# Causal mask of both attentions: from TensorE products to one fused VectorE pass

## The chip, the cores and the metric

The kernel runs on one core of a Trainium2 chip. The metric is the device time of one execution in microseconds, as the median of several runs. The engines of the core work in parallel, each in its own program order: TensorE (PE in the profile, its weight loads PEld), VectorE (DVE), ScalarE (ACT), GpSimd (POOL) and SyncE (SP), which issues most of the DMAs. They wait for one another by counting semaphores that the kernel sets.

## The reference

A decoder trunk of two layers, 512 tokens of width 1024, everything in float32. A layer projects the normalised input to four token mixers (a block attention A, an RWKV-7 recurrence B, a gated spatial unit C and a differential attention D), projects their outputs back, and adds a mixture of 32 experts. The change concerns the scores of A and D:

```python
# A: with 512 tokens in blocks of 256 and up to 3 past blocks chosen, every past block is
# chosen, so this is plain causal attention with 4 heads of width 64
mask = mc[..., None] & (kpos <= pc[None, None, :, None, None])
s = jnp.where(mask, s, -jnp.inf)
p = softmax(s)

# D: two score maps of width 32 for each of 4 heads
mask = jnp.arange(end)[None, :] <= (q0 + jnp.arange(DIFF_Q_BLOCK))[:, None]
p = jax.nn.softmax(jnp.where(mask, s, -jnp.inf), axis=-1)
attn = p[:, :, 0] - lam * p[:, :, 1]
out = attn @ v
```

## The kernel before

Each layer has a projection stage, a mixer stage, the output projection with the routing, and the experts. In the mixer stage the function `mixer_steps` writes out by hand one order for all engines. It goes through the RWKV steps of two channel halves, c = 0 and c = 1. For each half these are P (products within a chunk), T (turns), V (a triangular solve of 16 x 16 blocks on VectorE, followed by a DMA round trip of the blocks through DRAM), L (merging of blocks), four times Z, B, S (the recurrence over chunks), F and, for c = 1, G (the end). Between these steps it places the units of the attentions, by the list `UNITS_PER_STEP`: A has 16 units (4 query tiles i of 128 rows times 4 heads) and D 16 more. A unit of tile i has w = 128 (i + 1) key columns. Units A0 to A6 lie beside the last steps Z to F of the first half, A7 to A10 beside P, A11 and A12 beside T, A13 on and D0 beside V, D1 to D3 beside L, D4 to D15 beside the steps Z, B, S of the second half. Each engine issues its part of the step and then its part of the unit. The steps V, Z and B of the second half also hold products on TensorE whose result is not used (`keep_busy`, L592).

In the function `attn` every engine does its share of unit u, and, behind it, of the units u - 1 and u - 2:

- TensorE: scores of unit u into one of two PSUM banks (L721; for D two maps, one in each bank, behind each other), the mask as a product of the identity and the constant `causal`, added to the diagonal block of the bank (L724; for D twice, after both maps), then the turning of the probabilities of unit u - 1 (L731), then the product with V of unit u - 2 (L743). The scores of u wait until the exponential has read the bank.
- VectorE: for unit u - 1 the reciprocal of the sums (L1395), for D also the combination of the two maps (L1398, L1400, L1401); then the negated maximum of unit u (L1408), once per map; then the output of unit u - 2 (L1415 for A, L1417 for D).
- ScalarE: the exponential of unit u with that maximum as bias, with the sum of the row as accumulator output (L1091), then the copy of the turned probabilities (L1099).

Before unit 0 of each attention TensorE turns the queries and keys (L707) and ScalarE copies them (L1081). From then on the key columns of the token buffer `TK[0]` are no longer read. GpSimd applies the rotary embedding to the inputs of D (L1713 to L1718) and later writes two identity buffers for the second half (L1736), waiting for the last output of the first half. SyncE fetches the expert weights: `fill(0)` after the second DMA round trip of the blocks, the next ones after `mixed_done`, which VectorE gives after the end of attention D, and most of them after the output projection.

Of the kernel before, what the change touches and what calls it, by code (L numbers as in the profile page):

```python
# [14 lines left out]
P = 128  # L15
# [42 lines left out]
    fin_inA=4, fin_psA=3, fin_sqA=1, y_doneA=1, fin_inD=4, fin_psD=3, fin_sqD=1, y_doneD=1,  # L58
    mixed_done=1, mt_ps=6, mt_a=4, mt_v=2, res_ps=8, res_added=8, n2_squares=4, n2_turned=4, n2_copied_a=4, n2_copied_v=4,
    logits=4, exp_in=2, exp_done=2, chosen=2, ranks=2, routed=2, xt_ps=15, xt_copied=16, gate_ps=32, up_ps=32, gated=32, hidden=32,  # L60
    ht_ps=32, ht_copied=32, y2_ps=32, y2_copied=33, combined=8, first_hot=4, picked=3, lam_rt=3, sgu_done=1)

OV_ADDS = dict(ov_in=(0, 48), ov_used=(2, 1), ov_made=(6, 7), ov_ps=(0, 15), ov_gated=(0, 1), ov_copied=(0, 6), ov_added=(5, 8))

# [21 lines left out]
def build(nc, x, w_in, w_out, pcol, prow, w2a2, g2, sguT, router, norm2_g, w_gate, w_up, w_down,  # L86
          final_g, cf, cm, out):
    ctx = ExitStack()
    with ctx:
# [47 lines left out]
        def cst(name):  # L137
            lo, n = CF[name]
            return CFs[:, lo:lo + n]
# [32 lines left out]
        QKV = {"A": TK[0], "D": TK[2]}  # L172
        BLOCK_TO = [TK[0], TK[1], TK[3], TK[2]]
        VAD, UV = TK[1], TK[3]
        XS = XSb[:, :].rearrange("p (g t) -> p g t", g=8)
        AR = view(SC, 0, 2048, "p (c m w t) -> p c m w t", c=2, m=4, w=2)
        BT = view(SC, 2048, 1024, "p (c t) -> p c t", c=2)
# [114 lines left out]
        extra_full = [sem(f"extra_full{m}") for m in range(4)]  # L292
        combined = sem("combined")
        first_hot, picked = sem("first_hot"), sem("picked")
        lam_rt, sgu_done = sem("lam_rt"), sem("sgu_done")

# [68 lines left out]
        with nc.Block() as block:  # L367
# [143 lines left out]
            def _(pe):  # L511
# [4 lines left out]
                for layer in range(DEPTH):  # L516
# [180 lines left out]
                    def attn(m, u):  # L697
# [12 lines left out]
                        if u < 16:  # L710
                            i, h = unit_of[u]
                            w = (i + 1) * P
                            for a in range(nm):
                                n = u if m == "A" else 2 * u + a
                                if n >= 2:
                                    pe.wait_ge(*at(layer, s["exped"], n - 1))
                                if m == "A":
                                    rows = slice((h % 2) * 64, (h % 2) * 64 + 64)
                                else:
                                    rows = slice((h % 2) * 64 + a * 32, (h % 2) * 64 + a * 32 + 32)  # L720
                                mm(PS[5 + n % 2][:, 0:w], QKT[rows, h // 2, i * P:w], QKT[rows, 2 + h // 2, 0:w], start=True, stop=False)  # L721
                            for a in range(nm):
                                n = u if m == "A" else 2 * u + a
                                mm(PS[5 + n % 2][:, i * P:w], ident, cst("causal"), start=False, stop=True).then_inc(s["scores"], 1)  # L724
                        if 1 <= u <= 16:
                            i, h = unit_of[u - 1]
                            pe.wait_ge(*at(layer, s["exped"] if m == "A" else s["probs"], u))
# [228 lines left out]
            def _(act):  # L956
# [25 lines left out]
                for layer in range(DEPTH):  # L982
# [92 lines left out]
                    def attn(m, u):  # L1075
                        s, nm = mix[m], 2 if m == "D" else 1
                        if u == 0:
                            scale = float(HD) ** -0.5 if m == "A" else 32.0 ** -0.5
                            for j in range(4):
                                act.wait_ge(*at(layer, s["qk_ps"], j + 1))  # L1080
                                ac(QKT[:, j, :], PS[5 + j % 2][:, :], ACT.Copy, scale=scale if j < 2 else 1.0).then_inc(s["qk_copied"], 1)  # L1081
                        if u < 16:
                            i, h = unit_of[u]
                            w = (i + 1) * P
                            if u >= 2:
                                act.wait_ge(*at(layer, s["pt_ps"], u - 1))
                            for a in range(nm):
                                n = nm * u + a
                                col = (0 if m == "A" else 16) + n
                                act.wait_ge(*at(layer, s["maxed"], n + 1))  # L1090
                                ac(PB[:, u % 2, a, 0:w], PS[5 + n % 2][:, 0:w], ACT.Exp, bias=nmx[:, col:col + 1],  # L1091
                                   accum_out=sums[:, col:col + 1]).then_inc(s["exped"], 1)
                        if 1 <= u <= 16:
                            i, h = unit_of[u - 1]
                            w = (i + 1) * P
                            act.wait_ge(*at(layer, s["pt_ps"], u))
                            if u >= 3:
                                act.wait_ge(*at(layer, s["o_ps"], u - 2))
                            ac(PT[:, (u - 1) % 2, 0:w], PS[7][:, 0:w], ACT.Copy).then_inc(s["pt_copied"], 1)  # L1099
# [47 lines left out]
            def _(dve):  # L1147
# [47 lines left out]
                for layer in range(DEPTH):  # L1195
# [191 lines left out]
                    def attn(m, u):  # L1387
# [14 lines left out]
                        if u < 16:  # L1402
                            i, h = unit_of[u]
                            w = (i + 1) * P
                            for a in range(nm):
                                n = nm * u + a
                                dve.wait_ge(*at(layer, s["scores"], n + 1))
                                V.tensor_reduce(nmx[:, base + n:base + n + 1], PS[5 + n % 2][:, 0:w], AX.X, ALU.max, negate=True).then_inc(s["maxed"], 1)  # L1408
                        if u >= 2:
                            n = u - 2  # L1410
                            i, h = unit_of[n]
# [281 lines left out]
            def _(pool):  # L1693
# [11 lines left out]
                for layer in range(DEPTH):  # L1705
# [25 lines left out]
                    pool.wait_ge(*at(layer, proj_copied, copied("t", (3, NT - 1))))  # L1731
                    pool.wait_ge(*at(layer, sgu_ps, 1))
                    rope("D", SC0 + 11136, 16, 4)
                    pool.wait_ge(*at(layer, mix["A"]["y_ps"], 4))
                    for buf in (DB, EB):
                        G.tensor_copy(buf, eye).then_inc(mix["D"]["eye"], 1)  # L1736
# [133 lines left out]
```

## Time and profile before

| | us |
|---|---|
| median of 3 runs | 1950.47 (1950.07 to 1953.31) |
| the profiled execution, its own time | 1947.54 |
| its span in the profile, first to last instruction | 1945.7 |
| TensorE busy, whole span | 1665.0 |
| VectorE busy | 620.4 |
| ScalarE busy | 277.4 |
| GpSimd busy | 153.6 |

All times within the profile count from the start of the span. The mixer stage of layer 0 lies at about 228 to 375, that of layer 1 at about 1191 to 1338. An engine row gives start and duration of an instruction or of a group that follows without a break; what stands in brackets is the idle time of the engine just before it and the instruction whose end ended that idle time.

### The profile page before, as it was taken

The page shows a single profiled execution, that of the slowest core. Times are in us where ns is not written, and L with a number is a line of the kernel's source. Part 1 is how long each engine was busy: PE and PEld are TensorE (multiplying, and loading weights), DVE is VectorE, ACT ScalarE, POOL GpSimd, SP SyncE. Part 2 cuts the span into 40 slices and gives each one's busy share as a digit, 9 for nine tenths or more (in the row PEclk, how much of TensorE's full clock was granted, in tenths as well). Part 3 has the DMA queues.
Part 4 walks back from the last instruction along what each step waited for, and adds up shares of the span by engine and source line. Part 5 has one row for each costly group of instructions (what it writes and reads, how often), then busy time and mean ns, then how long its engine had stood idle before and what let it go on. Part 6 is the DMA issues. An engine that isn't in the chain of part 4 may idle for free.

```text
span 1945.7 us, 22555 instructions
## 1 busy us (share of the span) xinstructions
PE 1665.0 (86%) x9440; PEld 1005.9 (52%) x9440; DVE 620.4 (32%) x1397; ACT 277.4 (14%) x636; POOL 153.6 (8%) x171
## 2 busy tenths in 40 slices
PE   7999878899998878977599998788999988788872
PEld 4445557557665445544244465565576644455441
DVE  2164265715121113111313633566241211131113
ACT  2211233311000000000113113332100000000001
POOL 0010100002111110100001001000031111101100
PEclk9999999898999999999799999898989999899996
DMA  9212001056999999999822020101489999999994
GB/s 303 87 45 93 1 9 44 1 246 271 423 424 425 425 423 397 422 425 425 336 80 92 6 89 1 52 1 71 194 346 423 424 423 424 425 398 425 425 423 186
DMA packets 72772, 492.93 MB, mean 253 GB/s; under 512 B 24964, under 2 KB 26948, under 8 KB 36833
## 3 DMA queue, kind: packets, MB, share of 16 engines
q1 hardware_dynamic: 62592, 475.10, 59.4%
q0 software_dynamic: 10080, 16.41, 2.3%
q8 instruction: 75, 1.23, 0.3%
q14 instruction: 25, 0.20, 0.0%
HBM read 479.58 MB, written 28.11 MB: 261 GB/s over the span
## 4 chain that ended last, share of the span: by engine, by line
PE 62%; DMA 24%; DVE 7%; SPq 3%; issue 2%; ACT 1%; DVEq 0%; POOLq 0%; ACTq 0%
PE banks L844 13%; PE banks L552 12%; DMA RING<-in_w_up 8%; PE banks L859 7%; PE banks L797 6%; PE banks L541 6%; DMA RING<-in_w_down 6%; DMA RING<-in_w_gate 5%; DMA SCAN<-in_w_down 4%; PE banks L822 2%; PE banks L721 2%; SPq L434 2%; PE banks L743 1%; PE banks L632 1%; PE banks L649 1%
## 5 line engine op out<-in xcount | busy, mean ns | idle before, releaser
L844 PE MATMUL banks<-RING,XS 128*64 128x256 f32 x2816 | 326.5, 388 | 47.9 <-DMA RING<-in_w_up 31.2
L844 PEld LDWEIGHTS banks<-RING,XS 128*64 128x64 f32 x2816 | 224.8, 140 | 160.9 <-DMA RING<-in_w_up 42.2
L552 PE MATMUL banks<-RING,XNT 128*128 128x512 f32 x512 | 227.1, 601 | 0.2 <-DMA RING<-in_w_in_blocks 0.2
L859 PE MATMUL banks<-RING,XS 128*64 128x512 f32 x736 | 168.1, 597 | 26.9 <-issue 14.4
L1589 DVE SCALAR_TENSOR_TENSOR XS<-banks,TABLE,XS 128x256 f32<-128x256 f32 x60 | 29.0, 484 | 453.8 <-PE banks L844 453.3
L552 PEld LDWEIGHTS banks<-RING,XNT 128*128 128x128 f32 x512 | 97.8, 193 | 119.7 <-issue 118.6
L1130 ACT ACTIVATE XS<-banks,TABLE 128x256 f32<-128x256 f32 x60 | 28.5, 474 | 816.3 <-PE banks L844 816.3
L1780 POOL DMA_INDIRECT y_rows<-XS,SOLVE x64 | 64.9, 1014 | 631.1 <-DVE XS L1626 617.5
L844 PE MATMUL banks<-TOK,XS 128*64 128x256 f32 x768 | 92.5, 397 | 25.7 <-DMA SCAN<-in_w_down 11.1
L859 PEld LDWEIGHTS banks<-RING,XS 128*64 128x64 f32 x736 | 58.0, 136 | 105.2 <-issue 105.2
L1626 DVE COPY XS<-banks 128x512 f32<-128x512 f32 x64 | 44.2, 691 | 210.4 <-PE banks L859 210.4
L541 PE MATMUL banks<-XNT,RING 128*128 128x512 f32 x256 | 110.2, 592 | 0.0
L844 PEld LDWEIGHTS banks<-TOK,XS 128*64 128x64 f32 x768 | 63.7, 144 | 57.1 <-issue 23.0
L797 PE MATMUL banks<-RING,XNT 128*128 128x512 f32 x192 | 90.4, 617 | 1.4 <-ACT XNT L1104 1.4
L541 PEld LDWEIGHTS banks<-XNT,RING 128*128 128x128 f32 x256 | 48.6, 190 | 61.2 <-issue 61.2
L1091 ACT ACTIVATE XNT<-banks,SMALL 128x128 f32<-128x128 f32 (+3 forms) x96 | 50.1, 525 | 132.8 <-DVE SMALL L1408 127.6
L797 PEld LDWEIGHTS banks<-RING,XNT 128*128 128x128 f32 x192 | 37.1, 199 | 44.6 <-issue 42.4
L1408 DVE TENSOR_REDUCE SMALL<-banks 128x1 f32<-128x128 f32 (+3 forms) x96 | 44.1, 486 | 31.1 <-PE banks L724 30.2
L850 PE MATMUL banks<-CF,XS 128*128 128x128 f32 x132 | 30.2, 310 | 27.0 <-DVE XS L1589 23.4
L721 PE MATMUL banks<-XNT 32*128 32x128 f32 (+7 forms) x192 | 50.8, 476 | 2.7 <-ACT XNT L1081 2.7
L1354 DVE COPY_PREDICATED RING<-CM,banks 128x512 f32<-128x512 uint8 x40 | 29.2, 729 | 73.7 <-PE banks L647 43.1
L1744 POOL DMA_INDIRECT slot_table<-SMALL,SOLVE x16 | 15.8, 989 | 457.3 <-DVE SOLVE L1573 453.1
(312 smaller groups left out, 1950.8 us busy)
## 6 DMA issues: line engine op xcount, KB each, us to landing
RING<-in_w_up SPq DMA_DIRECT2D x46, 2048.0 KB, 27.4
RING<-in_w_down SPq DMA_DIRECT2D x46, 2048.0 KB, 27.2
RING<-in_w_gate SPq DMA_DIRECT2D x42, 2048.0 KB, 29.6
TOK<-in_w_gate SPq DMA_DIRECT2D x14, 2048.0 KB, 28.5
RING<-in_w_in_blocks SPq DMA_DIRECT2D x12, 2048.0 KB, 9.6
TOK<-in_w_up SPq DMA_DIRECT2D x10, 2048.0 KB, 33.4
TOK<-in_w_down SPq DMA_DIRECT2D x8, 2048.0 KB, 30.5
SCAN<-in_w_gate SPq DMA_DIRECT2D x6, 2048.0 KB, 19.0
```

The source lines that it names most:

```text
L434: sp.dma_start(dst, src.rearrange("a p n -> p (a n)")).then_inc(full, 16)
L541: last = mm(bank[:, :], w[:, k, j * P:(j + 1) * P], XNT[:, k, :], start=(k == 0), stop=(k == KD - 1))
L552: last = mm(bank[:, :], XNT[:, k, i * P:(i + 1) * P], w[:, k, :], start=(k == 0), stop=(k == KD - 1))
L721: mm(PS[5 + n % 2][:, 0:w], QKT[rows, h // 2, i * P:w], QKT[rows, 2 + h // 2, 0:w], start=True, stop=False)
L797: last = mm(PS[4 * n + i][:, :], src[:, i * P:(i + 1) * P], w[:, k, :], start=(k == 0), stop=(k == KD - 1))
L822: last = mm(PS[k // 4][:, (k % 4) * P:(k % 4 + 1) * P], X3[:, i, :].rearrange("t (p k) -> t p k", k=KD)[:, :, k], HOT[:, i, :], start=(i = ...
L844: last = mm(bank[f * CAP:(f + 1) * CAP, 0:256], rows[:, k, :], w[:, k, f * 256:(f + 1) * 256], start=(k == 0), stop=(k == KD - 1))
L859: last = mm(PS[5][n * CAP:(n + 1) * CAP, :], HT[:, j, f * CAP:(f + 1) * CAP], w[:, k, n * BN:(n + 1) * BN], start=(k == 0), stop=(k == KF ...
L1091: ac(PB[:, u % 2, a, 0:w], PS[5 + n % 2][:, 0:w], ACT.Exp, bias=nmx[:, col:col + 1], accum_out=sums[:, col:col + 1]).then_inc(s["exped"], 1)
L1408: V.tensor_reduce(nmx[:, base + n:base + n + 1], PS[5 + n % 2][:, 0:w], AX.X, ALU.max, negate=True).then_inc(s["maxed"], 1)
L1626: V.tensor_copy(YS[h], PS[5][:, :]).then_inc(y2_copied, 1)
L1780: pool.indirect_dma_start(y_halves, bass.IndirectOffsetOnAxis(ap=YROW[:, e:e + 1], axis=0), YS[h], None, bounds_check=4 * SEQ - 1, oob_is_ ...
```

## The change

The mask is no longer added by TensorE. The scores close their accumulation with the product L721 itself, so each map counts as ready by itself. VectorE runs one instruction per map over the bank: it adds a mask read from SBUF, multiplies by -1, writes the result back in place into PSUM, and folds the minimum of what it writes into the [128, 1] column that held the negated maximum before. The exponential reads the negated scores with a scale of -1. The mask is a tile of 4 blocks of 128 columns, three of zeros and one causal block, laid in the first key columns of `TK[0]`; a unit of tile i reads its last i + 1 blocks. GpSimd lays it once per layer, after its work on D's inputs and after TensorE has turned A's keys; VectorE waits for it ahead of unit A0.

```diff
@@ views and semaphores
+        MASK = TK[0][:, :, GW:GW + P]
...
+        mask_laid = sem("mask_laid")        # counted up to 2 in each layer
@@ TensorE, attn, u < 16
-                                mm(PS[5 + n % 2][:, 0:w], QKT[rows, h // 2, i * P:w], QKT[rows, 2 + h // 2, 0:w], start=True, stop=False)
-                            for a in range(nm):
-                                n = u if m == "A" else 2 * u + a
-                                mm(PS[5 + n % 2][:, i * P:w], ident, cst("causal"), start=False, stop=True).then_inc(s["scores"], 1)
+                                mm(PS[5 + n % 2][:, 0:w], QKT[rows, h // 2, i * P:w], QKT[rows, 2 + h // 2, 0:w], start=True, stop=True).then_inc(s["scores"], 1)
@@ ScalarE, attn
-                                ac(PB[:, u % 2, a, 0:w], PS[5 + n % 2][:, 0:w], ACT.Exp, bias=nmx[:, col:col + 1],
+                                ac(PB[:, u % 2, a, 0:w], PS[5 + n % 2][:, 0:w], ACT.Exp, scale=-1.0, bias=nmx[:, col:col + 1],
                                    accum_out=sums[:, col:col + 1]).then_inc(s["exped"], 1)
@@ VectorE, attn
-                                V.tensor_reduce(nmx[:, base + n:base + n + 1], PS[5 + n % 2][:, 0:w], AX.X, ALU.max, negate=True).then_inc(s["maxed"], 1)
+                                if (m, n) == ("A", 0):
+                                    dve.wait_ge(*at(layer, mask_laid, 2))
+                                sv = PS[5 + n % 2][:, 0:w].rearrange("p (b t) -> p b t", t=P)
+                                V.tensor_tensor_reduce(sv, sv, MASK[:, NT - 1 - i:NT, :], -1.0, -2 * NEG, ALU.add, ALU.min,
+                                                       nmx[:, base + n:base + n + 1]).then_inc(s["maxed"], 1)
@@ GpSimd, after rope("D")
+                    pool.wait_ge(*at(layer, mix["A"]["qk_ps"], 4))
+                    G.memset(MASK[:, 0:NT - 1, :], 0.0).then_inc(mask_laid, 1)
+                    G.tensor_copy(MASK[:, NT - 1, :], cst("causal")).then_inc(mask_laid, 1)
```

## Rows read from the trace of the kernel before

**Rows 1.** The chain that ended last, by engine, whole span (part 4 of the page).
```profile
PE 62%; DMA 24%; DVE 7%; SPq 3%; issue 2%; ACT 1%; DVEq 0%; POOLq 0%; ACTq 0%
```
**Rows 2.** Windows: length, busy us (count) per engine, clock, DMA share, GB/s.
```profile
225.00:330.00 105.00, 87.38 (x560) 65.60 (x558) 57.03 (x163) 38.79 (x111) 2.02 (x2) 0.95 0.08 25
...
520.00:1180.00 660.00, 564.52 (x3203) 320.19 (x3200) 163.88 (x292) 60.17 (x114) 52.76 (x52) 0.96 0.73 302
```
**Rows 3.** Line L724 on TensorE: duration in ns (least, median, most), all records.
```profile
L724 PE MATMUL banks<-CF x192: 275/275/377, 228.3 to 1325.3; 128*128 128x128 f32 x192
```
**Rows 4.** Order of time, TensorE: a mask product in A15 and one in D8.
```profile
275.78 0.49 PE L724 MATMUL banks<-CF 128*128 128x128 f32 x2
276.10 0.60 PE L731 MATMUL banks<-CF,XNT 128*128 128x128 f32 x4
...
333.45 0.71 PE L724 MATMUL banks<-CF 128*128 128x128 f32 x4
334.00 0.38 PE L731 MATMUL banks<-CF,XNT 128*128 128x128 f32 x2
```
**Rows 5.** Order of time, units A0 to A2: table load, VectorE's step, next RWKV step.
```profile
227.90 1.28 ACT L1091 ACT_TABLE_LOAD   x1
...
228.87 0.29 DVE L1408 TENSOR_REDUCE SMALL<-banks 128x1 f32<-128x128 f32 x1 [4.89 <-PE banks L724]
...
232.06 0.35 DVE L1369 SCALAR_TENSOR_TENSOR RING<-RING,SMALL,CF 128x128 f32<-128x128 f32 x1
...
232.58 0.61 PE L658 MATMUL banks<-RING 128*128 128x64 f32 x4
```
**Rows 6.** Order of time, VectorE, beside step P, unit A8.
```profile
250.61 1.74 DVE L1308 RECIPROCAL RING<-RING 128x256 f32<-128x256 f32 x1
...
252.59 0.56 DVE L1408 TENSOR_REDUCE SMALL<-banks 128x1 f32<-128x384 f32 x1
```
**Rows 7.** Order of time, VectorE, beside step V, unit A15.
```profile
276.37 0.69 DVE L1408 TENSOR_REDUCE SMALL<-banks 128x1 f32<-128x512 f32 x1 [0.94 <-PE banks L724]
277.58 0.28 DVE L1415 TENSOR_SCALAR TOK<-banks,SMALL 128x64 f32<-128x64 f32 x1 [0.51 <-PE banks L743]
```
**Rows 8.** Order of time, TensorE, unit A11: the turn waits for ScalarE.
```profile
261.93 0.52 PE L731 MATMUL banks<-CF,XNT 128*128 128x128 f32 x3 [0.43 <-ACT RING L1099]
```
**Rows 9.** Order of time, TensorE, beside step L: the turn waits for VectorE.
```profile
303.30 0.33 PE L731 MATMUL banks<-CF,XNT 128*128 128x128 f32 x1 [0.76 <-DVE XNT L1401]
```
**Rows 10.** Waits of VectorE from 318 to 364: us in all, times, longest.
```profile
DVE SMALL L1408 <- PE banks L724: 2.1, 6, 0.5
```
**Rows 11.** Order of time, VectorE, unit D7: two maxima in one row.
```profile
330.73 0.76 DVE L1408 TENSOR_REDUCE SMALL<-banks 128x1 f32<-128x256 f32 x2 [0.54 <-PE banks L724]
```
**Rows 12.** VectorE groups by shape, 225 to 375: count, busy us, mean ns, idle before.
```profile
L1408 DVE TENSOR_REDUCE SMALL<-banks 128x1 f32<-128x512 f32 x12 | 7.9, 686 | 2.0 <-PE banks L724 2.0
...
L1325 DVE TENSOR_TENSOR RING<-banks,CF 128x512 f32<-128x512 f32 x8 | 5.1, 681 | 0.4 <-PE banks L612 0.4
...
L1408 DVE TENSOR_REDUCE SMALL<-banks 128x1 f32<-128x128 f32 x12 | 3.1, 286 | 9.7 <-PE banks L724 9.6
```
**Rows 13.** Order of time, ScalarE, the two exponentials of D13.
```profile
355.49 0.69 ACT L1091 ACTIVATE XNT<-banks,SMALL 128x512 f32<-128x512 f32 x1 [2.20 <-DVE SMALL L1408]
356.08 0.19 ACT L1091 ACTIVATION_READ_ACCUMULATOR XNT<-banks,SMALL 128x1 f32 x1
356.17 0.68 ACT L1091 ACTIVATE XNT<-banks,SMALL 128x512 f32<-128x512 f32 x1
```
**Rows 14.** Order of time, GpSimd, its first work after D's rotary embedding.
```profile
237.43 2.02 POOL L1736 COPY RING<-CF 128x1024 f32<-128x1024 f32 x2 [13.59 <-PE banks L687]
```
**Rows 15.** Windows of 5 us as in rows 2: the D stage's least busy, and behind it.
```profile
335.00:340.00 5.00, 4.22 (x34) 3.07 (x33) 3.25 (x10) 2.35 (x9) 0.00 (x0) 1.00 0.00 0
...
365.00:370.00 5.00, 2.40 (x5) 0.60 (x4) 2.93 (x7) 3.03 (x5) 0.00 (x0) 1.00 0.00 0
370.00:375.00 5.00, 3.22 (x20) 3.12 (x21) 1.47 (x4) 0.60 (x1) 0.00 (x0) 0.80 0.00 2
```

More of the change, by code:

```diff
@@ L60 @@
     logits=4, exp_in=2, exp_done=2, chosen=2, ranks=2, routed=2, xt_ps=15, xt_copied=16, gate_ps=32, up_ps=32, gated=32, hidden=32,
-    ht_ps=32, ht_copied=32, y2_ps=32, y2_copied=33, combined=8, first_hot=4, picked=3, lam_rt=3, sgu_done=1)
+    ht_ps=32, ht_copied=32, y2_ps=32, y2_copied=33, combined=8, first_hot=4, picked=3, mask_laid=2, lam_rt=3, sgu_done=1)
 OV_ADDS = dict(ov_in=(0, 48), ov_used=(2, 1), ov_made=(6, 7), ov_ps=(0, 15), ov_gated=(0, 1), ov_copied=(0, 6), ov_added=(5, 8))
@@ L294, in build @@
         first_hot, picked = sem("first_hot"), sem("picked")
-        lam_rt, sgu_done = sem("lam_rt"), sem("sgu_done")
+        lam_rt, sgu_done, mask_laid = sem("lam_rt"), sem("sgu_done"), sem("mask_laid")
         PROJ = ([("t", (0, 0)), ("t", (0, 1))] + [("b", g) for g in range(8)] + [("t", (0, 2))] + [("l", n) for n in range(6)]
```

## The prediction, made before the changed kernel ran

> **What bounds the kernel now.** I read the chain first: TensorE holds 62% of it, DMA 24%, VectorE 7% [rows 1]. Then the stages. The stretch from 520 to 1180, mostly experts, has a DMA share of 0.73 (the next layer's projections and mixers, with little DMA, among it); the experts hold none of the edited instructions. The edit lies in the mixer stage, 225 to 330 [rows 2] and on to 375 in layer 0, with a DMA share of 0.08, and again some 963 us later in layer 1, with the same times within 0.1 us per unit. Whatever the mixers gain or lose passes to the end in full: SyncE's queue starts the bulk of the expert weights only after `mixed_done`, so a DMA-bound stage starts earlier by the same amount.
>
> In the mixer stage two recurrences are interleaved: RWKV steps and attention units, one to three units per step. For a unit TensorE forms scores (L721), adds the mask (L724), later turns the probabilities (L731) and multiplies by V (L743); VectorE takes the maximum (L1408); ScalarE the exponential (L1091). I read each engine's order of time to see who waits last, unit by unit.
>
> **Removed from TensorE.** 96 mask products, 192 records [rows 3]. By start to start the path pays 275.78 to 276.10, 0.32 us, for one product in an A unit, and 333.45 to 334.00, 0.55 us, for the two of a D unit [rows 4]. If TensorE were the bound throughout that would be 2 x 16 x (0.32 + 0.55) = 27.8 us. It is not, so I go through the stages of layer 0.
>
> *Units A0 to A6 (228 to 245), beside the last RWKV steps of the first half.* A0 and A1 gain 0.1: the exponential of A0 starts only when ScalarE's table load is done (227.90 + 1.28), and the turn in A1 waits for it. A2 gains 0.07: behind it the next RWKV step starts at 232.58 and needs VectorE's L1369, which ends at 232.41 [rows 5]. A3, A4, A5 and A6 stand between steps whose copies are ready long before, and TensorE runs without a gap: 4 x 0.32 = 1.28. Together 1.45 us.
>
> *Units A7 to A10 (245 to 260), beside the products P.* VectorE is the bound: its instructions stand end to end, a 1.74 us reciprocal, then the short L1395, then the maximum at 252.59 without idle [rows 6]. TensorE's saving is worth nothing; a longer VectorE instruction costs in full, four times.
>
> *Units A11 to A15 (260 to 281), beside the triangular solve V.* TensorE is continuous from about 262 (keep-busy products among them), and VectorE waits for it: 0.94 us at 276.37 and 0.51 at 277.58 [rows 7, 8], just ahead of the last part of the solve, whose end starts the DMA round trip of the blocks. A11's product is hidden in the 0.43 that the turn waits for ScalarE at 261.93; A12 to A15 give 4 x 0.32 = 1.28 us. VectorE's slack of 0.5 to 0.9 us covers its own lengthening.
>
> *Units D0 to D3 (281 to 318).* Nothing: D0 lies in the DMA round trip, and for D1 to D3 the turn waits 0.76 us (as at 303.30, three times [rows 9]) for VectorE's L1401, which comes ahead of the maximum in VectorE's order.
>
> *Units D4 to D15 (318 to 364).* The loop here is mostly VectorE and ScalarE: L1395 and L1401 on unit u-1, maximum of the first map of u, two exponentials, L1395 again. TensorE enters only where VectorE waits for the mask: six waits, 2.1 us [rows 10], one of them the 0.54 ahead of 330.73 [rows 11]. Four lie in the loop (0.54, 0.54, 0.31, 0.20: 1.59). In the intervals with an S step the loop runs through L731, which waits for L1401 too: 333.45 would be left by 333.75 in place of 334.00, so 0.25, then 0.10 and 0.14 in two others. Together 2.08 us; I call a wait for a few tenths gone, because scores are then done before L1401.
>
> TensorE's side is 1.45 + 1.28 + 2.08 = 4.8 us a layer, 9.6 in both.
>
> **Added on VectorE.** 96 times a maximum over PSUM (0.286 us at 128 columns to 0.686 at 512) becomes a fused pass that reads PSUM and SBUF, writes PSUM and gives a minimum. No row of before shows one, nor VectorE writing PSUM. The element rate from the nearest rows: a two-input pass from PSUM at 512 takes 0.681 against the reduction's 0.686 [rows 12], so the streaming part is worth 0. For the extra output the nearest row is ScalarE's accumulator read, 0.19 us, of which 0.09 shows before the next instruction [rows 13]. Ends: minus 0.005 (no extra cost) and, if the two things are done one after the other, a whole further pass (+0.68 at 512); worked as in the slower rival below that end gives 11.1 us a layer against 4.8, 1963. I take +0.10 us each, d below, nearest to the accumulator row.
>
> The Trainium skill, page "VectorE: DVE Perf Modes", section "Two Vector instructions with no wait between them", says an instruction that also writes out an accumulator is two instructions, the pass and an accumulator read. It gives no duration for the second; with ScalarE's full 0.19 in its place the change would gain only 3 us, by the formula below, with its visible 0.09 some 7. No row of before shows VectorE doing it.
>
> On the path lie four of them (A7 to A10) and, in the D loop, the first map's pass in eight intervals (those without the S0 to S2 steps and F). The second map's pass then runs beside the first exponential. That cover is thin: the two exponentials follow each other by 0.68 us at 512 columns [rows 13], two maxima by 0.64. Past 0.04 us (512, three units), 0.06 (384, two) and 0.09 (256, three), d counts a second time. Cost per layer: 12 d + 8 d - 0.51 = 20 d - 0.5. At 0.10: 1.5 us, 3.0 in both.
>
> **Other edits.** The scale of -1 in the exponential is free. The mask tile: GpSimd, idle for 13.59 us ahead of 237.43 [rows 14], waits for the four turns (over by the 227.90 of [rows 5], since ScalarE's copies of them come before it), then sets 384 columns and copies 128. By its own two 1024-column copies at 2.02 us, an estimate of 0.6 us: laid near 228.3. The first maximum now begins at 228.87, and the exponential behind it not before the table load's end at 229.18 anyway, so some 0.5 us more is free. The added wait stands ahead of all VectorE work, but only once a layer. The next GpSimd work waits for y_ps and starts 9 us later; SyncE's queue is not touched.
>
> **Sum.** 9.6 - 3.0 = 6.6 us less. The profiled execution took 1947.54 (span 1945.7, 1.8 around it), so it would be 1940.9; the median of the runs, 1950.47, stands 2.9 above it, and on that scale I forecast 1943.9.
>
> **Rivals.**
> *The accumulator eats it.* d near 0.2 gives 9.6 - 7.0 = 2.6 us less, 1947.9: no change that can be told. For: 20 of them sit on the path per layer, and VectorE's rows have a large fixed part (0.286 us at 128 columns, of which the slope explains 0.13) that a second instruction could repeat. Against: the 0.19 of ScalarE shows only half.
> *Two cycles per element (slower).* Source and destination are the same PSUM bank. If each element costs its read and its write in turn, 512 columns take 0.686 + 0.533 = 1.22 us (the rows' slope is 0.400 us for 384 columns, 0.533 for 512). A7 to A10 lose 0.27 + 3 x 0.40 = 1.5; the eight D intervals, with both maps now exposed, 3 x 0.55 + 2 x 0.83 + 3 x 1.12 = 6.7; 8.1 a layer against 4.8: 6.6 us slower, 1957.1. It decides from d = 0.27 on average upward. For: no row shows such a pass. Against: rows from PSUM to SBUF run one element per cycle.
> *TensorE is the bound more often than I read.* Each unit gained early shifts the rest of its stage; half of the 27.8 would be 13.9 less the 3.0: 11 us less, 1939.5.
> *The clock.* From 368 TensorE waits for 3.3 us and the granted clock of 370 to 375 reads 0.80, some of it at the 1.2 GHz level [rows 15]. The Trainium skill, page "TensorE: Matmul & The Clock Gate", Part 1, holds that recent activity sets the clock, so removing products speaks against the change. In the D stage the slices of 5 us are busy for 4.22 (335 to 340, the least of them) to 5.0 at full clock, and the 2.40 at 365 still reads 1.00; taking out 0.7 should not drop it. If it did for one stretch of 8 us in each layer, the work there would take up to 4 us longer each, 8.0 in both against the 6.6: 1951.9, slower but within the bound.
>
> **Chances.** Forecast 0.48, more TensorE gain 0.08, accumulator 0.24, two cycles (or the whole further pass, a tenth of it) 0.14, clock 0.06. Beyond 0.2% (3.9 us, about what can be told from no change) the forecast needs d below 0.17; I give faster 0.57, same 0.26, slower 0.17. The range 1937 to 1957 reaches from most of the TensorE case to the two-cycle case; the forecast's own is 1940 to 1947.
>
> **What would show it.** The fused pass at 0.75 to 0.80 us at 512 columns; VectorE's waits for L721 near zero in 318 to 364; VectorE still busy end to end at 245 to 260 and slightly longer there; the solve's end 2 to 2.5 us earlier; the end of the D units 3.3 us earlier than now. Wrong if the pass takes over 0.95 at 512, if the clock reads 0.5 inside 230 to 365, or if the two stages gain and the expert stage gives it back.

## The result and the profile after

The changed kernel takes 2000.96 us (median of 4 runs, 1995.59 to 2003.98) against 1950.27 in the same comparison for the kernel before: a ratio of 1.0267 [1.0245, 1.0288], 50.7 us slower where 6.6 us faster was forecast. The profiled execution took 2000.45 us, span 1998.6. A few executions of some kernels here, at 2563 us and more, ran in a slow state and are left out of all comparisons. The chain that ended last hardly moved from [rows 1]:

```profile
PE 63%; DMA 24%; DVE 7%; SPq 3%; issue 2%; ACT 1%; DVEq 0%; POOLq 0%; ACTq 0%
```

The windows tell more (columns as in [rows 2], the granted clock is the third number from the end): the mixers of layer 0, its D stage, the experts, a stretch of the A units of layer 1, and layer 1's D stage.

```profile
225.00:330.00 105.00, 82.76 (x472) 60.81 (x468) 53.29 (x171) 35.63 (x98) 4.19 (x7) 0.84 0.08 25
330.00:395.00 65.00, 62.70 (x231) 40.39 (x231) 32.37 (x109) 20.35 (x65) 0.00 (x0) 0.53 0.00 1
520.00:1180.00 660.00, 563.89 (x3279) 318.97 (x3278) 164.90 (x289) 58.10 (x110) 59.60 (x63) 0.97 0.77 321
1230.00:1275.00 45.00, 37.41 (x207) 24.39 (x206) 33.84 (x99) 18.00 (x44) 2.03 (x2) 1.00 0.04 7
1313.00:1380.00 67.00, 65.43 (x236) 42.47 (x236) 33.19 (x114) 20.98 (x67) 0.00 (x0) 0.50 0.00 1
```

Both D stages ran at half the clock, the 1.2 GHz level, but for one slice of 5 us in layer 0 (0.84 in 350 to 355). I measure the stages from exponential to exponential on ScalarE: the A part from the first exponential to that of A15, the D stage from the first of D4 to the second of D15. These are the two ends of the D stage of layer 0 in the order of time of ScalarE:

```profile
329.37 0.47 ACT L1089 ACTIVATE XNT<-banks,SMALL 128x256 f32<-128x256 f32 x1 [2.84 <-DVE SMALL L1409]
...
393.54 0.68 ACT L1089 ACTIVATE XNT<-banks,SMALL 128x512 f32<-128x512 f32 x1
```

So 64.2 us, where the kernel before took 42.7. The same subtraction from the two profiles accounts for the whole difference of the spans, 52.9 us: up to the first exponential +2.7 (a fall of the clock to 0.66 at 135 to 145 us, in the projections), A part of layer 0 +4.4 (0.50 to 0.69 in 230 to 250), between the parts +0.7, **D stage of layer 0 +21.5**, up to the first exponential of layer 1 +1.0, A part of layer 1 **-1.4** (the clock is full there), between +0.4, **D stage of layer 1 +22.3**, the rest +1.3.

The edited instruction itself is cheap. VectorE's groups by shape, whole span, to be held against [rows 12]:

```profile
L1409 DVE CUSTOM_DVE_ANT_1 banks<-banks,TOK 128x512 f32<-128x512 f32 x24 | 16.4, 710 | 14.2 <-PE banks L722 14.0
L1409 DVE DVE_READ_ACCUMULATOR2_ANT SMALL<- 128x1 f32 x96 | 13.5, 141 | 0.1
L1409 DVE CUSTOM_DVE_ANT_0 banks<-banks,TOK 128x128 f32<-128x128 f32 x24 | 6.7, 308 | 17.4 <-PE banks L722 17.3
```

And two passes in one unit, order of time:

```profile
385.57 0.70 DVE L1409 CUSTOM_DVE_ANT_1 banks<-banks,TOK 128x512 f32<-128x512 f32 x1 [1.47 <-PE banks L722]
386.19 0.14 DVE L1409 DVE_READ_ACCUMULATOR2_ANT SMALL<- 128x1 f32 x1
386.19 0.73 DVE L1409 CUSTOM_DVE_ANT_1 banks<-banks,TOK 128x512 f32<-128x512 f32 x1
```

The second pass starts 0.62 us behind the first; two maxima followed each other by 0.64. The accumulator read is there as an instruction of 0.14 us, but lies beside the next pass.

Now the place where the clock falls, TensorE in order of time, the turn and what stands behind it (L729, L722 and L593 are the turn, the scores and the keep-busy product):

```profile
324.56 0.48 PE L729 MATMUL banks<-CF,XNT 128*128 128x128 f32 x1 [1.40 <-DVE XNT L1399]
...
326.01 1.59 PE L593 MATMUL banks<-CF 128*128 128x384 f32 x2
327.53 1.22 PE L722 MATMUL banks<-XNT 32*128 32x256 f32 x4
```

The wait of 0.76 us of [rows 9] has become 1.40: the two mask products that filled some 0.6 of it are gone, and L1399 isn't earlier. Behind it the keep-busy product of 384 columns (two records) takes 1.59 us; at full clock a row of s7 below has 0.81. VectorE now waits for TensorE, where [rows 10] had 2.1 us in six waits (waits of VectorE from 325 to 394: us in all, times, longest):

```profile
DVE banks L1409 <- PE banks L722: 16.2, 9, 2.8
```

### The profile page after: what moved, and what is told of

Read it like the earlier page. It is cut to its first block, busy times and chain, and to the rows that moved or that the text cites. A ratio compares the mean times of both kernels' runs of the same rounds, so it can differ in the third digit from the quotient of the medians.

```text
span 1998.6 us, 22273 instructions
## 1 busy us (share of the span) xinstructions
PE 1708.6 (85%) x9248; PEld 1026.0 (51%) x9248; DVE 625.5 (31%) x1493; ACT 278.0 (14%) x636; POOL 155.1 (8%) x175
## 4 chain that ended last, share of the span: by engine, by line
PE 63%; DMA 24%; DVE 7%; SPq 3%; issue 2%; ACT 1%; DVEq 0%; POOLq 0%; ACTq 0%
PE banks L842 12%; PE banks L553 11%; DMA RING<-in_w_up 8%; PE banks L857 7%; PE banks L795 6%; DMA RING<-in_w_down 6%; PE banks L542 5%; DMA RING<-in_w_gate 4%; DMA SCAN<-in_w_down 4%; PE banks L722 2%; PE banks L741 2%; PE banks L820 2%; PE banks L729 2%; PE banks L593 1%; SPq L435 1%
## 5 line engine op out<-in xcount | busy, mean ns | idle before, releaser
L842 PE MATMUL banks<-RING,XS 128*64 128x256 f32 x2816 | 323.4, 385 | 49.4 <-DMA RING<-in_w_up 33.5
L857 PE MATMUL banks<-RING,XS 128*64 128x512 f32 x736 | 173.1, 612 | 28.9 <-issue 13.6
L842 PE MATMUL banks<-TOK,XS 128*64 128x256 f32 x768 | 91.1, 393 | 24.3 <-DMA SCAN<-in_w_down 11.4
L842 PEld LDWEIGHTS banks<-TOK,XS 128*64 128x64 f32 x768 | 62.9, 142 | 55.2 <-issue 22.4
L722 PE MATMUL banks<-XNT 32*128 32x128 f32 (+7 forms) x192 | 69.5, 674 | 2.7 <-ACT XNT L1079 2.7
L729 PE MATMUL banks<-CF,XNT 128*128 128x128 f32 x160 | 39.6, 357 | 29.7 <-DVE XNT L1399 18.9
L741 PE MATMUL banks<-TOK,RING 128*128 128x64 f32 x320 | 58.4, 330 | 2.5 <-DVE TOK L1417 1.7
L729 PEld LDWEIGHTS banks<-CF,XNT 128*128 128x128 f32 x160 | 21.5, 170 | 74.2 <-DVE XNT L1399 28.0
L741 PEld LDWEIGHTS banks<-TOK,RING 128*128 128x128 f32 x320 | 57.6, 259 | 3.0 <-issue 1.6
L795 PEld LDWEIGHTS banks<-RING,XNT 128*128 128x128 f32 x192 | 36.3, 194 | 43.3 <-issue 41.3
```

Source lines behind the costliest of these rows:

```text
L729: last = tr(PS[7][:, b * P:(b + 1) * P], PB[:, (u - 1) % 2, nm - 1, b * P:(b + 1) * P], ident)
L741: last = mm(PS[0][:, 0:HD], PT[:, n % 2, b * P:(b + 1) * P], VAD[:, b, v0:v0 + HD], start=(b == 0), stop=(b == i))
L795: last = mm(PS[4 * n + i][:, :], src[:, i * P:(i + 1) * P], w[:, k, :], start=(k == 0), stop=(k == KD - 1))
L842: last = mm(bank[f * CAP:(f + 1) * CAP, 0:256], rows[:, k, :], w[:, k, f * 256:(f + 1) * 256], start=(k == 0), stop=(k == KD - 1))
L857: last = mm(PS[5][n * CAP:(n + 1) * CAP, :], HT[:, j, f * CAP:(f + 1) * CAP], w[:, k, n * BN:(n + 1) * BN], start=(k == 0), stop=(k == KF ...
```

## The experiments

Each kernel is the changed one with one edit, unless it says "kernel before". Lengths are in us, from the exponentials as above, layer 0 / layer 1, in the profiled execution of each, which is a single one and can lie off the median (s7 1999.7, s9 1990.6, s13 1967.8, s17 1937.1). The ratio is to the kernel before, measured in the same comparison on the same chip; its median there was 1944.8 to 1946.6 us for s1 to s17, so ratios compare better than medians.

| kernel | A part | D stage | median | ratio |
|---|---|---|---|---|
| before | 48.0 / 48.0 | 42.7 / 42.7 | 1950.3 | 1 |
| changed | 52.4 / 46.6 | 64.2 / 65.0 | 2001.0 | 1.0267 [1.0245, 1.0288] |
| s1_same_products | 48.0 / 48.1 | 59.5 / 51.2 | 1979.7 | 1.0180 [1.0150, 1.0210] |
| s2_products_in_gap | 49.5 / 53.3 | 42.5 / 42.5 | 1950.8 | 1.0044 [1.0016, 1.0073] |
| s3_drop_only | 55.8 / 52.5 | 65.0 / 65.0 | 2040.5 | 1.0483 [1.0455, 1.0510] |
| s4_pass_only | 48.1 / 48.1 | 42.9 / 42.9 | 1947.3 | 1.0001 [0.9981, 1.0021] |
| s5_gap_D_only | 49.4 / 49.4 | 42.5 / 42.5 | 1950.4 | 1.0026 [1.0009, 1.0043] |
| s6_gap_A_only | 50.0 / 48.0 | 65.2 / 65.2 | 1998.9 | 1.0271 [1.0239, 1.0302] |
| s7_gap_D1_D3 | 55.9 / 52.7 | 55.2 / 61.8 | 1989.9 | 1.0216 [1.0194, 1.0237] |
| s8_gap_D4_on | 49.4 / 49.4 | 42.5 / 46.7 | 1962.0 | 1.0093 [1.0068, 1.0118] |
| s9_gap_half | 56.0 / 52.7 | 41.7 / 69.5 | 1981.8 | 1.0174 [1.0154, 1.0193] |
| s10_elsewhere | 51.3 / 46.6 | 47.0 / 48.7 | 1965.4 | 1.0110 [1.0086, 1.0134] |
| s11_before_less_idle | 48.0 / 48.0 | 41.2 / 41.2 | 1941.6 | 0.9984 [0.9959, 1.0009] |
| s12_gap_D_and_V | 55.5 / 54.8 | 42.5 / 42.5 | 1952.9 | 1.0022 [1.0002, 1.0042] |
| s13_gap_D_less_idle | 55.9 / 55.9 | 45.3 / 41.3 | 1952.7 | 1.0037 [1.0014, 1.0061] |
| s15_A_products_back | 48.0 / 48.0 | 42.5 / 42.5 | 1944.4 | 0.9994 [0.9981, 1.0007] |
| s16_both | 48.0 / 48.0 | 41.3 / 41.3 | 1946.0 | 1.0012 [0.9988, 1.0035] |
| s17_before_less_idle_again | 48.0 / 48.0 | 41.2 / 41.2 | 1950.5 | 1.0020 [0.9994, 1.0046] |

### Products or pass: which half of the change costs

My theory: the clock falls because the mask products are gone. The rival: the fused pass is dear. Four kernels divide the change.

**s4_pass_only**: fused pass, mask products kept.
```
 mm(PS[5+n%2][:, 0:w], ..., start=True, stop=False)
 mm(PS[5+n%2][:, i*P:w], ident, cst("causal"), start=False, stop=True)   # kept
 V.tensor_tensor_reduce(...)                                              # as changed
```

> The kernel before with the fused pass in place of the maximum and the mask products kept (the mask is added twice, the results are the same). Clock theory: clock 0.95 to 0.96 and the bare price of the pass, 0.07 us on some 12 to 20 places a layer: 1.7 to 3 us over the kernel before, 1952 to 1954. Pass rival: 1995 to 2003.

Measured 1.0001; each part of the table is 0.1 to 0.2 us longer. The rival falls.

**s3_drop_only**: kernel before, mask products away, plain maximum kept; it leaves the mask out, so its values are not those of the reference.
```
-mm(PS[5+n%2][:, i*P:w], ident, cst("causal"), start=False, stop=True)
```

> The kernel before with its 96 mask products left out and nothing put in their place: VectorE's maximum is the old reduction, the mask is not applied at all. Clock theory: slow like the changed kernel, 1990 to 2003, clock about 0.92. Pass rival: faster than before, 1935 to 1945, clock 0.95 to 0.96.

Measured 2040.5, 4.8% or some 94 us over the kernel before, without any fused pass. Both D stages are 65.0 us, as in the changed kernel, and the A parts lost clock too. But not all of it lies in the mixers: by the profiled execution 60 us lie there, and 33 between the last exponential of layer 0 and the first of layer 1 (861.0 for 828.1), where the changed kernel loses 1.0. What happens in that stretch is open, and with other values in it I don't use it. The window over the D stage of layer 0:
```profile
335.00:400.00 65.00, 63.43 (x229) 40.62 (x229) 31.03 (x87) 19.70 (x65) 0.00 (x0) 0.50 0.00 1
```

**s2_products_in_gap**: as many identity products of 128 columns as the mask had, into the bank of the turn, between the scores and the wait for the probabilities.
```
 if u >= 2:
     pe.wait_ge(*at(layer, s["pt_copied"], u - 1))   # stood behind the wait below
+for _ in range(nm):
+    mm(PS[7][:, 0:P], ident, cst("causal"), start=True, stop=True)
 pe.wait_ge(*at(layer, s["exped"] if m == "A" else s["probs"], u))
```

> The changed kernel with as many identity products (one per A unit, two per D unit), but written to the turn bank after the scores, ahead of the wait for the probabilities, and then overwritten by the turn. VectorE need not wait for them. Clock theory: clock 0.95 to 0.96 and time 1946 within 4, so some 4 us under the kernel before, since the six waits of VectorE in the D units (2.1 us a layer) go. Pass rival: 1995 to 2003. If position matters more than amount (products in the gap work, ahead of the scores don't), this one is fast and the one before it slow.

Useless work in an idle gap brings the ratio from 1.0267 to 1.0044, some 43 us. Both D stages are 42.5 us, shorter than the 42.7 before the change. The time, 1950.8, is just above the range I gave, and 5.5 us above the kernel before of its comparison where I had put 4 below: what is left, 0.44%, lies mostly in the A parts (49.5 and 53.3 us for 48.0, below).

**s1_same_products**: an identity product ahead of each score product, in its bank, overwritten by the scores.
```
+mm(PS[5+n%2][:, i*P:w], ident, cst("causal"), start=True, stop=True)
 mm(PS[5+n%2][:, 0:w], QKT[rows, ...], QKT[rows, ...], start=True, stop=True)
```

> The changed kernel with the same number of identity products of 128 columns put back on TensorE, now ahead of each score product in its bank, which overwrites them: the fused pass stays, the mask still comes from VectorE. Clock theory (the loss is TensorE running at its lower clock level, because products that kept it busy are gone): granted clock back to 0.95 to 0.96, D units of layer 0 take about 46 us in place of 70, time 1951 within 4. Rival, the fused pass (PSUM written in place, accumulator read) costs it: stays at 1995 to 2003. Rival, the order (TensorE now stands idle longer ahead of the turn of the probabilities, 1.40 against 0.76 us): the idle stays as long, so it stays slow, above 1980.

A miss: 1979.7. The clock is 1.00 until 365 us in layer 0 and still the stage is long. TensorE in order of time says why:
```profile
339.97 0.91 PE L723 MATMUL banks<-XNT 32*128 32x384 f32 x2
340.81 0.49 PE L722 MATMUL banks<-CF 128*128 128x128 f32 x2
341.22 0.91 PE L723 MATMUL banks<-XNT 32*128 32x384 f32 x2
```
```profile
325.00:365.00 40.00, 40.00 (x217) 26.04 (x217) 26.43 (x92) 15.33 (x51) 0.00 (x0) 1.00 0.00 1
```

### Where in the mixers, and how much

**s5 to s8**: the gap products of s2 with a condition: `m == "D"`, `m == "A"`, `m == "D" and u <= 3`, `m == "D" and u > 3`.

> The changed kernel with two idle identity products of 128 columns in every D unit, between the scores and the wait for probabilities; none in A units. Clock theory: the loss of 50 us lies in the D stages (first exponential of D4 to last of D15 takes 64.2 and 65.0 us at half clock against 42.7 and 42.7), so they come back to 42 to 44 us with a granted clock of 1.0 in most of the stage, and the time to 1952 +- 8; what is left over is the stretch of A0 to A5 at 0.5 to 0.7 (52.3 us against 48.0 in layer 0). Rival, that the A units are where the trouble starts: 1990 or more.

> The same with one product in every A unit and none in D units. Clock theory, D seat: D stages stay at 64 to 65 us, the time 1997 +- 6. Rival, that the clock is lost in the A units and only carried into D: D stages come back, 1955 +- 8.

> Two products in the units D1 to D3 of each layer alone, which go beside the L steps, where TensorE sat idle 1.40 us before each turn (0.76 before the change) and right behind which its clock fell to 0.50 at 324.2 us. If the entry decides (once at full clock TensorE keeps it, since D4 to D15 leave it busy 4.2 us of 5 or more): D stages 41 to 44 us in both layers, 1952 +- 10, as with products in all D units. If what D4 to D15 themselves lost decides: still 60 us or more each, 1990 or more.

> Two products in D4 to D16 of each layer alone, none beside the L steps. If the entry decides: the clock falls at the L steps as before and the D stages stay at 60 us or more (the products add to it at half clock, 0.6 us per unit): 2000 +- 10. If D4 to D15 decide: the clock comes back within the stage, 45 to 50 us each, 1965 +- 10.

s5 and s6 met their clock-theory numbers: nearly all of the 50 us lies in the D stage. s7 refutes what I had thought from the fall at 324 us: the entry doesn't decide. Both layers entered the D stage at full clock and lost it, layer 0 some 18 us in and layer 1 some 8. Its stages, 55.2 and 61.8 us, and its time, 1989.9, stand just short of the 60 and 1990 of the other reading. s8 took 1962.0, as forecast; its layer 0 entered at full clock, with no products beside the L steps, and kept it (42.5 us). This is TensorE in layer 0 of s7, in order of time, with the turns of four units:
```profile
338.38 0.41 PE L732 MATMUL banks<-CF,XNT 128*128 128x128 f32 x2 [0.70 <-DVE XNT L1402]
...
341.91 0.41 PE L732 MATMUL banks<-CF,XNT 128*128 128x128 f32 x2 [1.22 <-DVE XNT L1402]
...
343.27 0.81 PE L593 MATMUL banks<-CF 128*128 128x384 f32 x2
...
347.85 0.41 PE L732 MATMUL banks<-CF,XNT 128*128 128x128 f32 x2 [0.28 <-DVE XNT L1402]
...
352.53 0.52 PE L732 MATMUL banks<-CF,XNT 128*128 128x128 f32 x3 [1.52 <-DVE XNT L1402]
...
354.00 1.31 PE L593 MATMUL banks<-CF 128*128 128x384 f32 x2
```
At full clock most of the freed time has become waits for the probabilities, and behind the wait of 1.52 the clock is gone (0.92 in 350 to 355, 0.50 from 355 on). s8 shows the other side: its layer 1 entered its stage at half clock (0.54 in 1285 to 1300) and, with products in every unit, came back after three units: 4.59, 5.08 and 5.50 us from unit to unit, then 3.01.

**s9_gap_half**: `range(1)` for `range(nm)` in D units.

> The changed kernel with one idle product of 128 columns in each D unit (half of what the mask products were), in the same gap. If the clock is lost by a matter of amount, half may or may not do: kept throughout, the D stages are 42.0 to 42.5 us and the time 1946 to 1952; lost for a part of the stage only, one or both stages stand between 45 and 60 us and the time between 1955 and 1985; half clock throughout, 1995 or more. I expect the middle one, 1968. A rival in which any product between scores and turn keeps the clock, whatever its size, expects the first.

Layer 0 kept the clock throughout, in 41.7 us, the first D stage a full microsecond below that of before; layer 1 entered at half clock and stayed there to the end, 69.5 us. The time, 1981.8, is within the range of my middle case, but no stage is: one shows the first case and one the last. In this one execution half the filling left it to the clock at which the stage was entered.

**s10_elsewhere**: none in the gaps, 24 products of 128 columns a layer in the scan steps instead.
```
 keep_busy(PS[2], 3 * P)
+for _ in range(3):
+    keep_busy(PS[2], P)        # and so for PS[1] in step B
```

> The changed kernel with the 24 products of 128 columns that D4 to D15 of a layer lost put into the scan steps (three behind each product that already keeps TensorE busy in the Z and B steps of the second chunk), and none in the units. If the amount of work in the stage decides, wherever it stands: clock 1.0 in most of the D stage, D4 to D15 in 42 to 45 us, 1960 +- 10 as with the products in D4 to D16. If their place between scores and turn decides (what they delay there): 60 us or more each and 1995 or more.

In between: 1965.4 us is within the first range, but the stages, 47.0 and 48.7 us, are longer than the 42 to 45 given. The clock goes down and comes back within the stage (0.66 in 345 to 350).

**s11_before_less_idle**: kernel before, without its own eight idle 384-column products in the Z and B steps of the second chunk.
```
-if c:
-    keep_busy(PS[2], 3 * P)    # and PS[1] in step B
```

> The kernel before, mask products and plain maximum kept, without the idle 384-column products of the Z and B steps (8 per layer, 0.86 us each, 6.9 us of TensorE). Clock theory: the clock falls in the D stage as it does in the changed kernel though nothing of the mask is changed, D4 to D15 60 us or more, 2000 +- 20. If only the changed masking brings the loss: the stage gets no longer and the time is 1930 to 1950.

The clock-theory number, 2000, missed by 58 us. Eight products of 384 columns are as many columns as the 24 mask products of 128 that D4 to D15 lose, and the clock stays at 1.00. The theory in the form "less work, lower clock" is wrong. Four windows over D units at full clock (kernel before, s11 and s5 over 25 us, s7 over the 14 ahead of its fall) show a difference:

```profile
324.00:349.00 25.00, 23.72 (x167) 16.81 (x167) 17.24 (x52) 11.44 (x40) 0.00 (x0) 1.00 0.00 1
```
```profile
323.00:348.00 25.00, 23.26 (x163) 16.96 (x161) 17.86 (x55) 11.43 (x40) 0.00 (x0) 1.00 0.01 1
```
```profile
331.00:356.00 25.00, 23.72 (x169) 16.78 (x167) 17.70 (x66) 11.41 (x40) 0.00 (x0) 1.00 0.01 1
```
```profile
336.00:350.00 14.00, 11.74 (x84) 7.79 (x82) 10.24 (x42) 6.92 (x27) 0.00 (x0) 1.00 0.01 1
```

TensorE stands idle for 1.28, 1.74 and 1.28 us of 25 in the three that keep the clock, and for 2.26 of 14 in the one that loses it. The eight products stood partly on the path: without them the stage shrank by 1.5 us. Seven of them lie inside it and took 5.4 us there from start to start; the idle time that the profile shows grew by 0.3 only (1.88 in 42.5 us, 2.15 in 41.2), and the rest went into groups that start later one behind the other, the scores above all (eleven groups, 9.6 us from their starts to the next ones before, 11.4 without). These look like waits of a few tenths that the view counts as busy, which isn't shown. The mask products mostly stood in the shadow of the wait for VectorE: without them the waits ahead of the turns become longer.

**s13_gap_D_less_idle** puts this to the test: the gap products of s5, and the eight products away.

> The changed kernel with two products of 128 columns in the gap of each D unit, and without the eight idle 384-column products of the Z and B steps. If what decides is that TensorE does not stand idle before the turns, and not how much filling there is: clock 1.0 in D4 to D15 and 41 to 42 us for them, as in the kernel before without those eight (41.2 us), time 1947 +- 5 (1950.4 with the eight, less 2 x 1.3). If the amount decides: the clock falls in the D stage, 50 us or more, 1965 or more.

The D stage of layer 1 took 41.3 us at clock 1.00 (by amount, it should have fallen). That of layer 0 lost the clock at 350 and had it back at 362, and took 45.3: a miss. The fall came behind a wait no longer than that of the same unit in s11, 0.79 us in both:
```profile
348.91 0.55 PE L728 MATMUL banks<-CF,XNT 128*128 128x128 f32 x3 [0.79 <-DVE XNT L1398]
```
The median, 1952.7, is just above what I gave (at most 1952), the executions spread from 1945 to 1973, wider than those of s5 (1943 to 1959), and the profiled one is among the slower. The amount rival fails too (1965 or more). So the run speaks against amount alone and against idle time alone.

### The A parts

With full D stages 0.3 to 0.4% is still missing.

**s12_gap_D_and_V** added one `keep_busy(PS[7], 3 * P)` in the gap of the A units from the eleventh on.

> A candidate: the changed kernel with two products of 128 columns in each D unit and one of 384 in each A unit from the eleventh on (beside the V steps, where TensorE waits 2.1 us for each turn and the clock fell to 0.51 at 265 to 275 us with products in D alone). Clock theory: the fall there goes, the last three gaps between A exponentials come from 6.09, 3.99 and 3.44 us to about 4.6, 3.5 and 3.4, and the time to 1945 +- 5. If the fall only moves to another stretch: 1950 +- 4, no better than without.

The fall at 265 us went and another came, at 230 to 250 and 1190 to 1215, in and ahead of the first A units; the time is 1952.9: "moves to another stretch" was right.

**s15_A_products_back**: mask products back in their place for A units, fused pass everywhere, gap products in D units.
```
 if m == "D": mm(scores, ..., stop=True)
+else:
+    mm(scores, ..., stop=False)
+    mm(PS[5+n%2][:, i*P:w], ident, cst("causal"), start=False, stop=True)
```

> The changed kernel with the mask products of the A units back in their place behind each score product (the fused pass kept), and two gap products in the D units. If the falls of the clock in the A part (0.51 at 265 to 275 us and 0.56 at 1230 us with gap products in D alone, 49.4 us from first exponential to A15's against 48.0 before) come from the mask products that left the A units: none there, 48.0 to 48.2 us, and the time 1946 +- 3. Rival, that they come from elsewhere: they stay, 1950 +- 3.

Met: 48.0 us in both layers, no fall in either A part, 0.9994. The window over the first A part:
```profile
230.00:290.00 60.00, 53.99 (x323) 37.84 (x323) 37.98 (x121) 25.83 (x66) 2.76 (x5) 1.00 0.03 6
```

**s16_both** takes the eight products away too, and **s17** repeats s11.

> Both of these: mask products in the A units, gap products in the D units, the eight idle products of each layer's Z and B steps away. Clock kept throughout by the idle theory: 1943 +- 4, no better than the kernel before without the eight (1941.6). By the amount theory as s13: 1965 or more.

> The kernel before without the eight idle products, once more, since 0.9984 with an interval of 0.9959 to 1.0009 left open whether it is faster: by its trace, 41.2 against 42.7 us in D4 to D15 of each layer, 3 us, 1942.5, ratio 0.9985.

The D stages are 1.4 us shorter in each layer, as expected, and s16's 1946.0 is in its range. Yet s17 missed by 8 us: its ratio is 1.0020 [0.9994, 1.0046] after s11's 0.9984 [0.9959, 1.0009]. The profiled executions are among the fastest (1937.1 and 1935.9), but others of both reach 1962. What they lose, and where, is not in a trace here. None of the versions is measurably faster than the kernel before.

## Why the prediction was wrong, point by point

**The step that failed is the clock rival**, "taking out 0.7 should not drop it", and its price, "for one stretch of 8 us in each layer". It had the chance of 0.06. It happened in both layers, over nearly the whole of D4 to D15: +21.5 and +22.3 us, not 4. The A part of layer 0 and the projections ahead of it lost another 4.4 and 2.7 to the clock. Two readings led there. I looked at whether slices of 5 us were well filled at full clock (4.22 of 5, [rows 15]) and treated the rest as room; and I had worked out myself, in the stages further up, that most of the freed time in D1 to D15 would turn into waiting for VectorE (0.55 us freed a unit, 2.08 gained in twelve units, so 4.5 us of new idle time a layer in D4 to D15 alone). The two were never put together. That sum was the warning: 4.5 us more idle time in a stage of 43 us that idled for some 2 (1.28 in 25 us by the window above). For the price I also took the clock to come back by itself after one stretch. In the changed kernel, and in layer 1 of s9, it stays at half clock but for one slice: TensorE is then busy nearly all the time, at 1.2 GHz. It did come back within the stage in s8, s10 and s13, but not in s1.

On this the Trainium skill, "TensorE: Matmul & The Clock Gate", section "A second HAM failure mode: psum-queue depth-cycling", describes a kernel in which short but frequent idle spells between groups of matmuls make the clock go down and up again. The first half agrees with s7 (waits of 0.70, 1.22 and 1.52 us, then the fall), but not with the A part of layer 1 of the changed kernel (waits up to 1.47 us at 1.00) nor with s1 (a fall without a wait); the second with s10 and s8's layer 1, but not with the changed kernel's D stages, which came back for one slice only (0.84 at 350 to 355).

**TensorE's side, 4.8 us a layer**: right in kind where the clock held, but too large. The A part of layer 1 ran at full clock and took 46.6 us for 48.0: 1.4 us gained, against 2.73 less 0.4 for the four passes, 2.3. Between exponentials A0 to A6 gave 0.56 us of 1.45, A6 to A11 cost 0.05 where 0.4 was put, and A11 to A15 gave 0.86 of 1.28: the path was less often TensorE's than I read. From D3 to D8, s7's layer 0 at full clock took 15.1 us where the kernel before took 16.1: 1.0 of the 2.08 in five of twelve units; the interval behind them, mostly at full clock too, was 0.2 longer than before. A whole D stage of the changed kernel at full clock is in no trace.

**VectorE's side, d = 0.10**: mis-sized, to the good. s4 gives it by itself: D stage +0.16 us and A part +0.15 a layer, 0.3 for the 1.5 in the sum. By my 20 instructions on the path this is some 0.015 us each. The fused pass at 512 columns reads 0.710 (0.75 to 0.80 foretold). The two-cycle rival (1.22 us) and the accumulator rival (d of 0.2) are both refuted by the rows. The rule of the Trainium skill cited in the prediction ("VectorE: DVE Perf Modes", "Two Vector instructions with no wait between them"), two instructions for an accumulator output, agrees with the trace: 96 accumulator reads for 96 passes, 0.141 us each and hidden beside the next pass.

**The mask tile**: GpSimd's two instructions, 0.42 and 0.29 us, at 230.06, ended 0.5 us before the first fused pass needed them. Right.

```profile
230.06 0.42 POOL L1737 MEMSET TOK<- 128x384 f32 x1 [3.47 <-PE banks L708]
230.41 0.29 POOL L1738 COPY TOK<-CF 128x128 f32<-128x128 f32 x1
...
231.20 0.30 DVE L1409 CUSTOM_DVE_ANT_0 banks<-banks,TOK 128x128 f32<-128x128 f32 x1 [4.47 <-PE banks L722]
```

**What would show it wrong**: I had written "if the clock reads 0.5 inside 230 to 365". It did.

**My first correction was wrong too**: "the clock follows the amount of work" fell with s11, "the entry decides" with s7. What stands is narrower. In the D units the mask products kept TensorE's clock: without them it falls, in both layers (changed kernel, s3, s6), and with as many products ahead of the wait for the probabilities the D stages take 42.5 us (s2, s5, s12, s15). Idle time ahead of the turns is the difference that these traces show most plainly, but it doesn't decide by itself, and three rows say so: the A part of layer 1 of the changed kernel held 1.00 over 45 us with 7.6 of them idle, waits of 1.41 and 1.47 us among them; s13's layer 0 fell behind waits of 0.49 and 0.79 us that s11 bore; s1's layer 0 fell with no wait shown. These are two turns of that A part, TensorE in order of time:

```profile
1240.28 0.41 PE L729 MATMUL banks<-CF,XNT 128*128 128x128 f32 x2 [1.41 <-ACT RING L1097]
...
1247.17 0.52 PE L729 MATMUL banks<-CF,XNT 128*128 128x128 f32 x3 [1.47 <-ACT RING L1097]
```

What decides is open. Open too: why half the filling held in one layer and not in the other, why the falls of the clock in the A parts move between places, and what the slower executions of s11 and s17 lose.

## What to carry to other kernels

Before taking work off TensorE, split it in two: what stands on the path, and what stands in the shadow of a wait. Taking out the second brings nothing, and it may be what keeps the clock. If the sum says "off the path", work out the price of the whole stage at 1.2 GHz as well; the cheapest trial is to put idle products of the same size back into the gap. A replacement is best tried in halves (the new pass with the old products, the old pass without them): here two runs showed one half free (1.0001) and the other dear (1.0483).

## What the runs showed of the hardware that I had not expected

- At half clock TensorE can be shown busy without a break (by the modelled ends of its matmuls) and not get its clock back: s9, layer 1, 70 us. In s8, layer 1, also nearly without a break at half clock, it came back after three units.
```profile
1297.00:1367.00 70.00, 70.00 (x251) 46.01 (x249) 31.66 (x108) 19.04 (x62) 0.00 (x0) 0.50 0.00 1
```
- VectorE reads and writes the same PSUM bank in one pass, with a second operand from SBUF and an accumulator, at the pace of the plain maximum: 0.62 us from pass to pass at 512 columns, 0.64 for the maxima.
- Two products in different 32-row strips cost as one (0.92 us for both at 384 columns, kernel before), and twice that (0.91 each, s1) with one over 128 rows between them.
